# Four more chunk pairs of the up projection computed with seven products instead of eight

## What is computed

```python
hn = rmsnorm(x, norm_ffn_pre[l])
u = jnp.square(jax.nn.relu(jnp.einsum('bsd,df->bsf', hn, w_up[l])))   # 2048 -> 8192
y = jnp.einsum('bsf,fd->bsd', u, w_down[l])                           # 8192 -> 2048
x = x + rmsnorm(y, norm_ffn_post[l])
```

## Time and profile before

| | |
|---|---|
| median of 3 runs | 2559.31 us |
| profiled execution, time | 2559.44 us |
| profiled execution, span | 2557.7 us |
| PE busy | 2551.5 us (100%) |
| DVE busy | 1764.6 us (69%) |
| ACT busy | 1296.9 us (51%) |
| granted PE clock | 1.000 |
| the DMA queue that loads weights | 68.3% of 16 engines |

### The profile page before, as it was taken

How to read it: one execution, slowest core, us unless ns; L and a number is a source line. 1 busy time by engine, 2 the same in 40 slices (tenths; PEclk the granted TensorE clock), 3 DMA queues, 4 the chain that set the end, 5 groups by cost and what they waited for, 6 DMA issues and landing times.

```text
span 2557.7 us, 29454 instructions
## 1 busy us (share of the span) xinstructions
PE 2551.5 (100%) x11425; PEld 2115.1 (83%) x11425; DVE 1764.6 (69%) x2062; ACT 1296.9 (51%) x1554; POOL 34.8 (1%) x56
## 2 busy tenths in 40 slices
PE   9999999999999999999999999999999999999999
PEld 7888888888888888888888888888888888888887
DVE  5646565566666666776876777678678768778686
ACT  6554443444555555455454544445465455455463
POOL 1000000000000000000000000000020000000000
PEclk9999999999999999999999999999999999999999
DMA  8767766676776777778566787666757677666674
GB/s 271 216 189 210 205 202 196 190 208 204 215 220 196 215 196 200 219 227 230 165 181 181 206 223 201 203 206 198 244 174 223 195 216 212 215 196 224 204 231 141
DMA packets 534795, 527.42 MB, mean 206 GB/s; under 512 B 294896, under 2 KB 297824, under 8 KB 534656
## 3 DMA queue, kind: packets, MB, share of 16 engines
q1 hardware_dynamic: 531856, 518.09, 68.3%
q0 software_dynamic: 2384, 6.93, 1.1%
q10 hardware_dynamic: 416, 0.52, 0.1%
HBM read 488.24 MB, written 2.10 MB: 192 GB/s over the span
## 4 chain that ended last, share of the span: by engine, by line
PE 100%; ACT 0%; DVE 0%; issue 0%; ACTq 0%
PE bank L2312 30%; PE bank L2313 30%; PE bank L2314 30%; PE bank L2379 2%; PE bank L2380 2%; PE bank L2381 2%; PE bank L2498 1%; PE bank L2487 1%; PE bank L2477 1%; PE bank L2411 0%; PE bank L2420 0%; PE bank L2433 0%; PE bank L2426 0%; PE bank L2558 0%; PE bank L2545 0%; PE bank L2578 0%
## 5 line engine op out<-in xcount | busy, mean ns | idle before, releaser
L1255 DVE TENSOR_TENSOR t_wl<-t_stage,t_wh 128x1024 fp32r<-128x1024 f32 x844 | 1021.4, 1220 | 600.2 <-ACT t_wh L714 594.8
L714 ACT ACTIVATE t_wh<-t_stage 128x1024 fp32r<-128x1024 f32 x845 | 885.1, 1057 | 801.4 <-PE bank L2314 758.3
L2312 PE MATMUL bank<-t_wl,t_xth 128*128 128x512 f32 x2400 | 941.0, 392 | 0.5 <-DVE t_xtl L1297 0.5
L2314 PE MATMUL bank<-t_wh,t_xtl 128*128 128x512 f32 x2400 | 934.1, 389 | 0.0
L2313 PE MATMUL bank<-t_wh,t_xth 128*128 128x512 f32 x2400 | 934.0, 389 | 0.0
L2314 PEld LDWEIGHTS bank<-t_wh,t_xtl 128*128 128x128 f32 x2400 | 450.5, 188 | 94.1
L2312 PEld LDWEIGHTS bank<-t_wl,t_xth 128*128 128x128 f32 x2400 | 450.6, 188 | 93.9 <-DVE t_xtl L1297 0.9
L2313 PEld LDWEIGHTS bank<-t_wh,t_xth 128*128 128x128 f32 x2400 | 450.7, 188 | 92.5 <-issue 0.2
L2312 PE MATMUL bank<-t_wl,t_yth 128*128 128x512 f32 x914 | 355.6, 389 | 0.0
L2313 PE MATMUL bank<-t_wh,t_yth 128*128 128x512 f32 x914 | 355.1, 389 | 0.0
L2314 PE MATMUL bank<-t_wh,t_ytl 128*128 128x512 f32 x914 | 355.1, 389 | 0.0
(11 more groups left out here) (410 smaller groups left out, 1509.4 us busy)
## 6 DMA issues: line engine op xcount, KB each, us to landing
t_stage<-in_a_w_in_dram SPq DMA_DIRECT2D x192, 512.0 KB, 4.3
t_stage<-in_w_in_dram SPq DMA_DIRECT2D x168, 512.0 KB, 4.3
t_stage<-in_b_w_in_dram SPq DMA_DIRECT2D x128, 512.0 KB, 4.5
t_stage<-in_w_up_dram SPq DMA_DIRECT2D x92, 512.0 KB, 4.4
t_stage<-in_w_down_dram SPq DMA_DIRECT2D x90, 512.0 KB, 5.1
t_stage<-in_a_w_out_dram SPq DMA_DIRECT2D x64, 512.0 KB, 4.3
t_ubuf<-in_w_down_dram SPq DMA_DIRECT2D x38, 512.0 KB, 5.3
t_ubuf<-in_w_up_dram SPq DMA_DIRECT2D x36, 512.0 KB, 4.5
```

The lines of the kernel that those rows point to most:

```text
L714: e.activation(wh[:, j % N_SPLIT], stage[s], ACT.Copy).then_inc(*hi(j))
L1255: e.tensor_tensor(low, src, high.bitcast(F32), ALU.subtract).then_inc(*lo(j))
L2312: e.matmul(o, h, w_l, start=start, stop=False)
L2314: return e.matmul(o, l, w_h, start=False, stop=stop)
```

## The change

`halved_pairs` takes chunks (q,2) and (q,3) of the up projection as pairs too, for all four q, so that only (0,0) and (0,1) stay plain. `groups_of` puts a pair's P2, P3 and P4 behind the first, second and third round of groups (a k, b k), for every pair of the kernel; before they stood behind (a,4), (b,4) and (a,6). In the programs of ACT, DVE and SP the evacuation of a paired up chunk is placed by the end of its unit: the transposes at the end + 1 and + 3, the squares at the end and + 2, the high and low parts at 9, 12, 5 and 8 positions behind the unit's end for chunks 0 to 3. The sums of the layer's input move ahead, directly behind the norm's scale. The row loads of the last norm wait for the last up pair's P3.

```diff
@@ -128,7 +128,7 @@ halved_pairs
-            [((kind, q, c), (kind, q, c + 1)) for q in range(4) for kind, c in (("up", 0), ("down", 0), ("down", 2))
+            [((kind, q, c), (kind, q, c + 1)) for q in range(4) for kind in ("up", "down") for c in (0, 2)
              if (kind, q, c) not in (("up", 0, 0), ("down", 3, 2))])
@@ -249,8 +249,7 @@ groups_of
         for n, k in enumerate((4, 6, 8, 10)):
-            own += [(a, k)] + {0: [(m, P2)], 1: [(m, P4)]}.get(n, [])
-            own += [(b, k)] + ([(m, P3)] if n == 0 else [])
+            own += [(a, k), (b, k)] + {0: [(m, P2)], 1: [(m, P3)], 2: [(m, P4)]}.get(n, [])
         return own + [(a, 12), (a, 14), (b, 12), (b, 14)]
@@ -289,9 +288,8 @@ low_after
-        if ("up", q, c) in pair_of:
-            return 8 if c == 0 else 10
-        return 8 if c == 3 else 4
+        behind = 4 if q == 0 and c < 2 else (9, 12, 5, 8)[c]
+        return behind + end("up", q, c if q == 0 and c < 2 else c | 1) - end("up", q, c)
...
@@ -1176,37 +1174,40 @@ scalar
+        def squared(q, c):
+
+            t = buf[c % 2]
+            if ("up", q, c) in pair_of:
+                slot(end("up", q, c | 1) + 2 * (c % 2))
+                e.wait_ge(*vec.at("sum", "up", q, c))
+            else:
+                slot(end("up", q, c))
+                e.wait_ge(*used.at(end("up", q, c) - 1))
...
         for q in range(4):
+            if q == 0:
+                slot(end("up", 0, 0) - 1)
+                sum_high("x3")
+            squared(q, 0)
+            if q == 0:
+                up_high(0, 0)
+            squared(q, 1)
+            apart(first_of["up", q, 2], turned.at("up", q, 0))
+            if q:
+                up_high(q, 0)
+            up_high(q, 1)
+            squared(q, 2)
+            squared(q, 3)
+            apart(first_of["down", q, 0], vec.at("late", first_of["down", q - 1, 2], 1) if q >= 2 else None)
+            up_high(q, 2)
             up_high(q, 3)
...
@@ -2140,30 +2141,34 @@ vector
         for q in range(4):
-            if ("up", q, 0) in pair_of:
-                for c in range(2):
-                    up_sum(q, c)
-                    up_turn(q, c)
+            if q:
+                up_sum(q, 0)
+                up_sum(q, 1)
+                up_turn(q, 0)
+                up_turn(q, 1)
+            else:
+                split_sums(xth, xtl, rowb.rearrange("p a b -> p (a b)"), vreg[:, 7168:8192], "x3")
+                slot(end("up", 0, 0))
+                sum_low("x3")
+                up_turn(0, 0)
+                up_low(0, 0)
+                up_turn(0, 1)
+            slot(end("up", q, 1) + 6)
+            together(first_of["up", q, 2], turned.at("up", q, 1))
+            if q:
                 up_low(q, 0)
-            else:
-                up_turn(q, 0)
-                up_low(q, 0)
-                slot(end("up", 0, 1))
-                split_sums(xth, xtl, rowb.rearrange("p a b -> p (a b)"), vreg[:, 7168:8192], "x3")
-                up_turn(q, 1)
-                slot(end("up", 0, 1) + 3)
-                sum_low("x3")
-                up_low(q, 1)
+            up_low(q, 1)
+            up_sum(q, 2)
+            up_sum(q, 3)
             up_turn(q, 2)
-            if ("up", q, 0) in pair_of:
-                up_low(q, 1)
+            up_turn(q, 3)
             up_low(q, 2)
+            up_low(q, 3)
+            slot(end("up", q, 3) + 9)
             if q:
                 late(first_of["down", q, 0])
             else:
                 together(first_of["down", q, 0])
-            up_turn(q, 3)
-            up_low(q, 3)
             down_evac(q, 0)
```

More of the change, by code:

```diff
@@ L613, in sync @@
             for c in range(4):
-                slot(end("up", q, c) + 1)
+                slot(end("up", q, c | 1) + 1 + 2 * (c % 2) if ("up", q, c) in pair_of else end("up", q, c) + 1)
                 send(flat[zt_buf[c]], quadrants(ytl, c), "up", q, c)
@@ L695, in gpsimd @@
         for c in range(4):
-            e.wait_ge(*(vec.at("dr", c - 2, 1) if c >= 2 else used.at(where[first_of["up", 3, 0], P3])))
+            e.wait_ge(*(vec.at("dr", c - 2, 1) if c >= 2 else used.at(where[first_of["up", 3, 2], P3])))
             load_row(c, A["norm_ffn_post_2"][:, cols(c)], "ffn", c)
@@ L1178, in scalar @@
         e.wait_ge(*vec.at("sF"))
-        for q in range(4):
[L1180 to L1195, removed]
-                else:
[L1197 to L1204, removed]
@@ new lines, in squared @@
+        def squared(q, c):
[6 more added lines that the diff above has]
+                e.wait_ge(*used.at(end("up", q, c) - 1))
+            for i in range(2):
+                e.activation(t[:, i, :], t[:, i, :] if ("up", q, c) in pair_of else accs("up", q, c)[i],
+                             ACT.Relu, scale=sF[:, i:i + 1]).then_inc(*act("up", q, c, i))
+            e.wait_ge(*act.at("up", q, c, 1))
+            e.activation(t, t, ACT.Square).then_inc(*act("squared", q, c))
@@ L1205, in scalar @@
             up_high(q, 3)
[L1206 to L1209, removed]
+            if q < 3:
+                apart(first_of["down", q, 2], vec.at("late", first_of["down", q, 0], 1) if q else None)
                 apart(first_of["up", q + 1, 0], turned.at("up", q, 2))
@@ L2142, in vector @@
         for q in range(4):
-            if ("up", q, 0) in pair_of:
-                for c in range(2):
-                    up_sum(q, c)
-                    up_turn(q, c)
-                up_low(q, 0)
-            else:
-                up_turn(q, 0)
-                up_low(q, 0)
-                slot(end("up", 0, 1))
-                split_sums(xth, xtl, rowb.rearrange("p a b -> p (a b)"), vreg[:, 7168:8192], "x3")
-                up_turn(q, 1)
-                slot(end("up", 0, 1) + 3)
-                sum_low("x3")
-                up_low(q, 1)
+            if q:
[13 more added lines that the diff above has]
+            if q:
+                up_low(q, 0)
+            up_low(q, 1)
+            up_sum(q, 2)
+            up_sum(q, 3)
             up_turn(q, 2)
-            if ("up", q, 0) in pair_of:
-                up_low(q, 1)
+            up_turn(q, 3)
             up_low(q, 2)
+            up_low(q, 3)
+            slot(end("up", q, 3) + 9)
             if q:
```

## The result

The changed kernel takes 2569.26 us (median; 2567.99 to 2569.47), the kernel before 2559.31 us beside it (2558.85 to 2560.19). The ratio is 1.0037, 95% interval 1.0027 to 1.0048: slower by 9.9 us. Forecast were 2564.5 us with a range of 2557 to 2571. The direction was right; 5.2 of the 9.9 us were forecast. The measured time lies in the stated range, near its upper end, and outside the forecast's own 2562 to 2567.

What follows compares the result with a forecast made beforehand. PE was taken to bound the kernel, busy 2551.5 of 2557.7 us. From the profiled 2559.44 us, -5.4 + 7.0 + 3.6 = +5.2 gave 2564.6, as a median 2564.5 us; range 2557 to 2571, the forecast's own 2562 to 2567.

Steps and rivals of the forecast that it cites:

- Term 1: Four more up pairs: 24 fewer matmuls at 0.2266 us each, 5.4 us less.
- Term 2: Start of the feed-forward layer: PE waits for DVE's low parts in the first up groups, 7.0 us more.
- The followed chain: Start of the layer: ACT's and DVE's instructions timed one behind the other from earlier rows, PE 7.0 us late.
- P6's wait of 1.7: Start of the layer: P6's low part done at 1914.2, PE wants P6 at 1912.5; a wait of about 1.7 us.
- g4: Fifth group of up chunk (0,1), counted from g0: low part done at 1905.7, wanted at 1902.8, PE waits 2.9 us.
- Term 3: Behind each quarter's up chunks: PE waits 0.9 us for up chunk 2's low part, four times, 3.6 us more.
- Other edits at 0: New place of P2 to P4, additional low parts and differences, later norm row loads: 0 beyond the terms.
- a8: Down pair group needing up chunk 2's low part: PE there at 13.6 us behind the unit's end, part done at 14.5.
- The fourth: Rival: DVE too full in q = 1 to 3, 1 to 2 us more for each quarter; 2569 us, chance 0.2.
- The second: Rival: only the layer's start holds PE, up chunk 2 is just in time; 2561.0 us, chance 0.19.
- the first: Rival: all is hidden, PE takes the 5.4 us and the lead holds; 2554.0 us, chance 0.08.
- the 0.5: Kernel before: PE's wait of 0.5 us at the start of the feed-forward layer, called its only one in that layer.

Runs made afterwards that it cites:

- experiment 10: Changed kernel with sums ahead of the norm's scale, chunk (0,0)'s transpose earlier, its high and low part later, and P2, P3, P4 at their old places: 2555.46 us.
- experiment 1: Changed kernel with the input sums ahead of the norm's scale, up chunk (0,0)'s transpose earlier and its high and low part later: 2562.41 us.
- experiment 6: Changed kernel with P2, P3 and P4 at their old places in the down pairs alone: 2561.92 us.
- experiment 2: Changed kernel with only the sums of the layer's input moved ahead of the norm's scale: 2566.04 us.
- experiment 5: Kernel before with only the new place of P2, P3 and P4, without new pairs: 2559.35 us.
- experiment 4: Changed kernel, new pairs kept, with P2, P3 and P4 at their old places in every pair: 2561.15 us.
- experiment 9: Changed kernel with the four differences of each pair made on 8 of 1024 columns, output not the reference's: 2563.40 us.
- experiment 3: Changed kernel with up chunk 2's high and low part one position earlier behind the unit's end: 2567.33 us.
- experiment 7: Changed kernel with P4 ahead of a8 in down pairs only, P2 and P3 at their new places: 2564.37 us.
- experiment 8: Changed kernel with P2 and P3 at their old places in down pairs only, P4 at its new late place: 2568.08 us.

## Why the prediction was right, and where it was short

- **Term 1 (-5.4): right.** 24 fewer matmuls, PE's busy time 5.4 us lower in experiment 10, which leaves nearly nothing else.
- **Term 2 (+7.0): right.** 6.97 by the start times. Taking it away gave 6.9, of which the start has 6.3 by the start times; that the median agrees so closely is in part luck (experiment 1). The followed chain hit each start to 0.15 us. One link was another: P6's wait of 1.7 was not there, since PE ran slower for 3.4 us and lost 1.6 in its place. In experiment 6 PE had the same wait of 2.6 us at g4, the clock stayed at 1.00, and P6's wait was there:

```profile
1905.47 0.50 PE L2321 MATMUL bank<-t_wl,t_xth 128*128 128x512 f32 x1 [2.55 <-DVE t_wl L1260]
1913.84 0.50 PE L2388 MATMUL bank<-t_wl,t_rsum 128*128 128x512 f32 x1 [1.27 <-DVE t_wl L1260]
```

 Its start lost 6.90 us, the changed kernel's 6.97. P6's deadline is set by DVE and the DMAs, so PE may lose the time in either way.
- **Term 3 (+3.6): right in place and sum, not in its parts.** Listed are 0.8, 1.3, 0.2 and 1.0 us for four times 0.9, 3.4 in all. The bounds (0 to 1.5 each) hold all four. DVE's queue, which I had as the last link, was that in q = 0; in q = 1 and 3 it was the DMAs, which I had at 5.6 us from the end of the transposes to ACT's start and which took 6.6. The close sum is partly luck: in the two kernels whose program is the same there, the four waits come to 2.2 us (experiment 1) and 2.6 (experiment 2), with the one in q = 1 at 0.5 and 0.8 for 1.3. Only q = 0 has 0.8 in all three.
- **Other edits at 0: this step failed.** Of the 7.9 us lost in the quarters 3.4 are the listed waits at a8, and 4.5 are not in the sum: about 1.0 for PE's restart behind these four (below), 2.6 for five short waits of 1.3 us and their restarts, and the rest, 0.9, in gaps that no row lists as a wait. The sentence "the new place of P2, P3 and P4 [...] moves no work between engines" is true and experiment 5 confirms it for the kernel before. But I priced the place by itself and then priced a8 with it. The old order would have brought PE to a8 at 14.96, behind the 14.5 at which I had the low part ready: by my own numbers it had the whole of term 3 in it, and the new place should have been charged with it. Experiments 4 to 6 show the size: 8.1 us for the place with the new pairs, 0 without. The short waits behind it I had put at up to 2 us for each of three quarters and then left out of the sum, though by my count DVE had 40 us of work in 42.2.
- **The rivals.** The fourth (DVE too full, 2569) has the time that was measured, but not the place: PE never waits in the up pairs for `t_mtl` or `t_yth`, but 3 to 50 us behind their end, in the down pair. Of its mechanism, slips of a full DVE, experiment 9 confirms a part, the 2.6 us of short waits; that its number fits is luck, since 1.0 us for restarts at a8 stands in no rival and experiment 4 takes all short waits away with DVE just as full. The second (only the start, 2561.0) is what experiment 4 made (2561.15), the first (all hidden, 2554.0) is nearly what experiment 10 made (2555.46). So terms 1 and 2 add as they were set up, and the miss lies behind the up pairs.
- **A wait passed over.** PE's list before also has 0.4 us for ACT (`t_cpb`) at the layer's end, where the prediction says that PE never waits but for the 0.5. It is the same in every run and changes nothing.
- **A wait costs more than its row.** The first matmul after a wait takes 0.50 us for 0.39, starts 0.15 later than the listed wait says, and the next starts 0.34 behind it for 0.227 (1895.98 to 1896.32). That is 0.25 us for each of the twelve new waits, 3 us that no list of waits has: 9.1 + 3.0 + 1.6 for the clock is 13.7 of the 14.9 us lost.

## What to carry to other kernels

An edit that costs nothing by itself can be the slack of another: when two edits meet at one deadline, work out the deadline with each of them undone, not only with both done. Follow the engine that feeds PE instruction by instruction for as long as its queue stays full, not only to the first wait: here the first 20 us of the layer were forecast to 0.15 us, while behind each up pair the queue was followed only to the first wait, and 4.5 us stood in no term. And when a wait is found, moving what PE does ahead of it (one product of 1.36 us, five us of the result) can do more than speeding up what it waits for.

## What the runs showed of the hardware

- After the wait of 2.5 to 2.6 us at g4 (and one of 1.2 us ten us before) the granted clock fell in the profiles of five of the six kernels that had it: 0.85 in the window from 1900 to 1910 in the changed kernel, 0.83, 0.83 and 0.83 in experiments 3, 7 and 8, about 3.4 us at the lower level; 0.75 with 0.91 in the next window in experiment 4, twice as long. In experiment 6 it stayed at 1.00 with the same waits. In the four kernels whose longest wait there was 1.5 us or less (experiments 1, 2, 9 and 10) it stayed at 1.00.
- In a kernel with such waits, whether it falls differs from one execution to the next. The mean granted clock is on record for every run. It is 1.000 in all runs of the kernel before and of experiments 1, 2, 5, 9 and 10, which leaves no room for half the clock over 3.4 us (1.7 of 2560 us is 0.0007). It is 0.999 in all five runs of the changed kernel. In experiments 3, 4, 6, 7 and 8 both occur: 5 of 7 runs, 5 of 10, 6 of 10, 8 of 11 and 5 of 6 have 0.999. In experiment 4 the two sorts of runs have the same median (2561.17 and 2561.13), in experiment 6 those with 0.999 take 0.3 us longer, in experiments 3, 7 and 8 0.9 to 1.4 us longer, from few runs. So what the fall costs in time is between nothing and its own 1.6 us. What decides it in one execution is open.
- The four small DMAs of one transposed chunk took SP 2.9 to 3.7 us to issue in the kernel before, where transposes of two chunks start at least 8.9 us apart. In the changed kernel a pair's start 4.8 to 5.9 us apart, and the issue took 3.0 to 4.2 us for the first chunk and 4.1 to 5.6 for the second (4.17 and 5.29 in the rows of q = 1). Whether the second set waits for the first in the queues or for the loads between them wasn't tried.
